# Expert weights loaded as pairs of tiles, one transfer each, on Trainium2

## The reference, cut to what matters

```python
def _moe_swiglu(h, router_w, router_b, w1, w3, w2):      # 8 experts, top 2, hidden width 2816
    logits = (h @ router_w).astype(jnp.float32) + router_b.astype(jnp.float32)
    top_vals, top_idx = lax.top_k(logits, TOP_K)
    ...
    for e in range(N_EXPERTS):
        out = out + gates[..., e:e + 1] * _swiglu(h, w1[e], w3[e], w2[e])
    return out
```

## Time and profile before

| what | value |
|---|---|
| device time, median of 3 runs | 4106.06 us (4105.6 to 4106.98) |
| the profiled execution, device time | 4107.23 us |
| its span, first to last instruction | 4105.4 us |
| mean granted TensorE clock | 0.922 |
| busy share PE, PEld, DVE, ACT | 87%, 75%, 66%, 49% |
| read from memory | 719.45 MB, 175 GB/s over the span |
| expert loads (`mraw`) | 726 of 512 KB, median 5.4 us to landing |

### The profile page before, as it was taken

One profiled execution on the slowest core, in us unless ns is written; L12 is line 12 of the kernel. 1 busy time (PEld: TensorE's weight loads), 2 busy tenths in 40 slices (PEclk: granted clock), 3 DMA queues, 4 the chain that ended last, 5 costly groups with the idle time before them and its releaser, 6 DMA issues.

```text
span 4105.4 us, 72288 instructions
## 1 busy us (share of the span) xinstructions
PE 3578.7 (87%) x27080; PEld 3085.1 (75%) x27080; DVE 2719.8 (66%) x3625; ACT 2028.4 (49%) x2685; POOL 145.8 (4%) x153
## 2 busy tenths in 40 slices
PE   7896629287999989899999999999997699997699
PEld 2374528286998976688888888887996599997598
DVE  6634765655555544789999999997556555555555
ACT  6622222212434433478888887886346244445343
POOL 0004900000000000000000000000000000000000
PEclk9897669699999999899999999999997699998699
DMA  9521000000454531179999999996542154543154
GB/s 354 211 87 46 1 6 3 1 3 30 147 182 153 180 138 52 66 258 360 365 363 360 364 360 363 360 362 223 182 159 92 47 184 154 189 157 109 46 169 159
DMA packets 199203, 723.08 MB, mean 176 GB/s; under 512 B 21872, under 2 KB 25328, under 8 KB 198640
## 3 DMA queue, kind: packets, MB, share of 16 engines
q1 hardware_dynamic: 198432, 713.89, 49.3%
q0 software_dynamic: 592, 6.69, 0.4%
HBM read 719.45 MB, written 1.05 MB: 175 GB/s over the span
## 4 chain that ended last, share of the span: by engine, by line
PE 80%; DVE 14%; ACT 3%; issue 1%; DMA 1%; SPq 0%; DVEq 0%; ACTq 0%; POOL 0%
PE ps L311 22%; PE ps L312 22%; PE ps L313 22%; PE ps L527 2%; DVE yc L2125 1%; PE ps L1268 1%; DMA ada_raw<-wstream 1%; PE ps L1265 1%; PE ps L1516 1%; PE ps L1533 1%; PE ps L1259 1%; PE ps L1848 1%; DVE rs L537 1%; PE ps L1797 1%; DVE normw L543 1%
## 5 line engine op out<-in xcount | busy, mean ns | idle before, releaser
L274 DVE TENSOR_TENSOR w_lo<-w_raw,w_hi 128x1024 fp32r<-128x1024 f32 x529 | 647.2, 1225 | 789.1 <-ACT w_hi L258 786.9
L311 PE MATMUL ps<-a_hi,w_hi 128*128 128x256 f32 (+1 forms) x3000 | 896.0, 299 | 94.0 <-DVE a_lo L1430 34.0
L258 ACT ACTIVATE w_hi<-w_raw 128x1024 fp32r<-128x1024 f32 x529 | 559.0, 1059 | 785.1 <-PE ps L313 762.1
L1933 DVE TENSOR_TENSOR mlo<-mraw,mhi 128x1024 fp32r<-128x1024 f32 x726 | 877.6, 1224 | 91.7 <-ACT mhi L1929 63.5
L312 PE MATMUL ps<-a_lo,w_hi 128*128 128x256 f32 (+1 forms) x3000 | 898.5, 299 | 0.0
L313 PE MATMUL ps<-a_hi,w_lo 128*128 128x256 f32 (+1 forms) x3000 | 896.0, 299 | 0.0
L1929 ACT ACTIVATE mhi<-mraw 128x1024 fp32r<-128x1024 f32 x726 | 770.7, 1062 | 180.7 <-PE ps L313 145.5
L311 PEld LDWEIGHTS ps<-a_hi,w_hi 128*128 128x128 f32 x3000 | 580.5, 194 | 120.2 <-issue 78.5
L313 PEld LDWEIGHTS ps<-a_hi,w_lo 128*128 128x128 f32 x3000 | 575.1, 192 | 16.2
L312 PEld LDWEIGHTS ps<-a_lo,w_hi 128*128 128x128 f32 x3000 | 574.4, 191 | 15.1
L311 PE MATMUL ps<-mhi,x_hi 128*128 128x512 f32 x968 | 395.9, 409 | 1.9 <-DVE mlo L1933 1.9
(11 more groups left out here) (489 smaller groups left out, 5226.3 us busy)
## 6 DMA issues: line engine op xcount, KB each, us to landing
mraw<-wexp SPq DMA_DIRECT2D x726, 512.0 KB, 5.4
w_raw<-wstream SPq DMA_DIRECT2D x529, 512.0 KB, 3.4
ada_raw<-wstream SPq DMA_DIRECT2D x96, 512.0 KB, 5.2
bia<-bias POOLq DMA_DIRECT2D x1, 4096.0 KB, 12.6
con<-consts SPq DMA_DIRECT2D x1, 1824.0 KB, 7.8
conb<-constsb POOLq DMA_DIRECT2D x1, 1224.0 KB, 7.5
hT<-ctxT SPq DMA_DIRECT2D x1, 1024.0 KB, 10.3
hT<-xT SPq DMA_DIRECT2D x1, 1024.0 KB, 12.5
```

Of the source, the lines that this page charges most:

```text
L258: nc.scalar.activation(whi[:, slot, :], raw[:, slot, :], ACT.Copy).then_inc(hi_ready.sem, 1)
L274: nc.vector.tensor_tensor(wlo[:, slot, :], raw[:, slot, :], whi[:, slot, :].bitcast(F32), ALU.subtract).then_inc(lo_ready.sem, 1)
L311: nc.tensor.matmul(out, lhs[0], rhs[0], start=start, stop=False, skip_group_check=skip)
L1933: nc.vector.tensor_tensor(mlo[:, slot, :], mraw[:, rslot, :], mhi[:, slot, :].bitcast(F32), ALU.subtract).then_inc(lo_ready.sem, 1)
```

## The change

The raw ring becomes three slots of two tiles (128 x 2048, 8 KB in a partition). One transfer of 1 MB loads a pair; its issue waits until DVE has finished both tiles of the pair that was there, and both tiles of a pair wait for the one semaphore of the slot. The host lays each two following tiles side by side. The bytes in SBUF, the bytes moved and the work of PE, ACT and DVE stay the same; 363 transfers take the place of 726.

```diff
-        mraw = sb("mraw", [P, MOE_RAW, 1024], at=x_at + 8 * KT * SLOTS)
+        mraw = sb("mraw", [P, MOE_RAW // 2, 2048], at=x_at + 8 * KT * SLOTS)
...
             def load(m, slot, idx):
                 if not (isinstance(m, int) and m < MOE_RAW):
-                    sp.wait_ge(lo_ready.sem, m + (BASE["moe"] - MOE_RAW + 1))
+                    sp.wait_ge(lo_ready.sem, m + (BASE["moe"] - MOE_RAW + 2))
                 sp.dma_start(mraw[:, slot, :], w[one(idx)].rearrange("o p c -> p (o c)")
                              ).then_inc(xraw[slot].sem, 16)
...
-                for q in range(4):
-                    load(m + q, (m + q) % MOE_RAW, e0 + q)
-                for q in range(2 if b else 0):
-                    load(m + 4 + q, (m + 4 + q) % MOE_RAW, before + (XT - 2 + q))
+                for q in range(2):
+                    load(m + 2 * q, (m // 2 + q) % (MOE_RAW // 2), e0 + q)
+                if b:
+                    load(m + 4, (m // 2 + 2) % (MOE_RAW // 2), before + (XT // 2 - 1))
                 with sp.Fori(0, NSTEP - 1) as i:
-                    for j in range(6):
-                        load(i * 6 + (b * XT + 4 + j), (4 + j) % MOE_RAW, i * 6 + (e0 + (4 + j)))
+                    for j in range(3):
+                        load(i * 6 + (b * XT + 4 + 2 * j), (2 + j) % (MOE_RAW // 2), i * 3 + (e0 + (2 + j)))
...
-            act.wait_ge(xraw[rslot].sem, rounds * 16 + (16 + ADA // ADA_RING * 16))
+            act.wait_ge(xraw[rslot // 2].sem, rounds * 16 + (16 + ADA // ADA_RING * 16))
             act.wait_ge(tile_used.sem, n)
-            nc.scalar.activation(mhi[:, slot, :], mraw[:, rslot, :], ACT.Copy).then_inc(hi_ready.sem, 1)
+            nc.scalar.activation(mhi[:, slot, :], mraw[:, rslot // 2, rslot % 2 * 1024:(rslot % 2 + 1) * 1024], ACT.Copy).then_inc(hi_ready.sem, 1)
...
-            nc.vector.tensor_tensor(mlo[:, slot, :], mraw[:, rslot, :], mhi[:, slot, :].bitcast(F32),
+            nc.vector.tensor_tensor(mlo[:, slot, :], mraw[:, rslot // 2, rslot % 2 * 1024:(rslot % 2 + 1) * 1024], mhi[:, slot, :].bitcast(F32),
                                     ALU.subtract).then_inc(lo_ready.sem, 1)
...
-    return np.concatenate(out + [o[-1]], 0)
+    out = np.concatenate(out + [o[-1]], 0)
+    return out.reshape(XT // 2, 2, P, D).transpose(0, 2, 1, 3).reshape(XT // 2, P, 2 * D)
```

More of the change, by code:

```diff
@@ L1664, in sp_experts @@
                 if b < NE:
-                    e0 = b * XT
+                    e0 = b * (XT // 2)
                 else:
@@ L1668, in sp_experts @@
                         sp.wait_ge(*S("overflow").next("sp"))
-                    e0 = sp.value_load(xi[0:1, b - NE:b - NE + 1], min_val=0, max_val=NE - 1) * XT
+                    e0 = sp.value_load(xi[0:1, b - NE:b - NE + 1], min_val=0, max_val=NE - 1) * (XT // 2)
                 m = b * XT - 2 if b else 0
-                for q in range(4):
-                    load(m + q, (m + q) % MOE_RAW, e0 + q)
-                for q in range(2 if b else 0):
-                    load(m + 4 + q, (m + 4 + q) % MOE_RAW, before + (XT - 2 + q))
+                for q in range(2):
+                    load(m + 2 * q, (m // 2 + q) % (MOE_RAW // 2), e0 + q)
+                if b:
+                    load(m + 4, (m // 2 + 2) % (MOE_RAW // 2), before + (XT // 2 - 1))
                 with sp.Fori(0, NSTEP - 1) as i:
-                    for j in range(6):
-                        load(i * 6 + (b * XT + 4 + j), (4 + j) % MOE_RAW, i * 6 + (e0 + (4 + j)))
+                    for j in range(3):
+                        load(i * 6 + (b * XT + 4 + 2 * j), (2 + j) % (MOE_RAW // 2), i * 3 + (e0 + (2 + j)))
                 before = e0
-            for q in range(2):
-                load(MOE - 2 + q, (4 + q) % MOE_RAW, before + (XT - 2 + q))
+            load(MOE - 2, 2, before + (XT // 2 - 1))
         def pe_router(pe):
```

## The result

The changed kernel takes 4152.48 us in the median (4150.7 to 4154.82, 4 runs) against 4106.36 us of the kernel before on the same chips (4105.6 to 4106.98, 4 runs). The ratio is 1.0112, 95% interval 1.0099 to 1.0124: 46 us slower. The forecast was 4176 us, 70 us slower.

What follows compares the result with a forecast made beforehand. PE was taken to set the expert stage's pace at 8.71 us a step; a pair's landing of 5.2 plus 4.1 us made it 9.3, and 119 x 0.59 = 70 us more gave 4176 us, range 4104 to 4295.

Steps and rivals of the forecast that it cites:

- the round: Expert stage: a raw slot's cycle from issue to issue, 8.0 us of an 8.71 us step before, 9.3 us after.
- The fixed part: Slot's round without landing: hand-overs of 0.15 and 0.1 us plus 3.8 us of ACT and DVE work, taken as 4.1 us.
- The limit for the landing: Expert stage: the pair's load stays hidden while its landing is under 8.71 - 4.1 = 4.6 us.
- the landing of 1 MB: L, a pair's time from issue to landing in the expert stage, taken as 5.2 us.
- the lone tiles: 512 KB loads in two other stretches, 3.2 and 4.2 us to land; their middle plus 1.28 us gave 5.0 us.
- The lower bound of 4.5: Landing of a pair at best: 3.2 us for a lone tile plus 1.28 us for the second 512 KB.
- Nothing else was to cost: Engine work and SP's issuing 0 us, the start 0 us, the end under 1 us; other stages the same.
- The spacing of the pairs: Expert stage loads: pairs issued 2.9 us apart and moving for 2.6 us, so they hardly queue behind each other.
- The signs: Expert stage trace if right: PE waits for mlo, ACT for even tiles' loads, blocks about 102 us apart, PE busy 93 to 95%.
- Hidden after all: Rival: the pair lands in 4.5 us and the step stays 8.6 to 8.7 us; 4102 to 4114 us, chance 0.16.
- The clock: Rival: PE's waits drop its clock to 1.2 GHz in half the steps, 4260 us; chance 0.06 together with the queue rival.
- The rival in which the queue of the loaded stage stays: Landing stays 6.7 us, step 10.8 us, 250 us more, 4356 us; chance 0.06 together with the clock rival.

Runs made afterwards that it cites:

- the joint landing alone: The kernel before, each tile's load issued as early as before, but the even tile's split also waits for the odd tile's landing; 4177.06 us, ratio 1.0178.
- The run with the gates moved: The changed kernel with the gate ahead of tile 0 and silu and product behind tile 3, on ACT and DVE; 4126.81 us, ratio 1.0053.

## Why the prediction was right, and where it was off

**What bounds the kernel, and the round**: right. The fixed part was worked out as 4.05 to 4.1 us from the trace of before; the chain shows 4.06 in the changed kernel and 4.03 with the joint landing alone. The 0.7 us that were said to be left in a round before are 0.77 in the mean. The limit for the landing, 4.6 us, is where the knee lies: a median of 4.5 us costs 7 us, one of 4.9 us costs 46. One refinement: the 8.71 us are a mean. The median round before is 8.58 us, and the step in which a block is spread (1.43 us more) makes up the rest, so in most steps the limit is nearer to 4.5.

**The term that was mis-sized** is the landing of 1 MB: "the middle of the lone tiles, (3.2 + 4.2) / 2 + 1.28 = 5.0, and 0.2 us for the load: 5.2 us". It was 4.9 us in the median and 5.13 in the mean. It is the mean that sets the pace here. By the median the sum would give 119 x 0.29 = 35 us, which is 11 us too few, because it leaves the late landings out. What makes a fifth of the pairs land late wasn't tried. For the two slots with the gate or silu between their tiles the means are 0.18 + 5.03 + 0.08 + 3.83 = 9.12 us; the forecast had 5.2 + 4.1 = 9.3. Of the 0.18 us between them 0.17 are the landing and 0.01 the rest, and 119 x 0.18 = 21 us are most of the 24 us by which the forecast was high.

The run with the gates moved shows what late landings cost by themselves. Its typical round in the chain is 8.53 us, just under PE's 8.58, and by its median landing of 4.8 us it would be hidden. But its mean landing is 5.06 and its mean round 8.87 us; 119 x (8.87 - 8.70) = 20 us is nearly all of its 21.

How L was put together was in part luck. No row stood for the 0.2 us "for the load", and the stretches of 3.2 and 4.2 us are from another stage. The runs give 3.8 us for 512 KB and 1.1 more for the second 512 KB in this stage, medians both, where 3.7, 1.28 and 0.2 were added. The lower bound of 4.5 was too low: nothing of 363 pairs landed under 4.6.

**Nothing else was to cost**: right. SP still waits for DVE for most of the stage (783 of 1000 us), its queue adds the same 0.18 us before an issue as it did, and the stage's 48 us are all of the 46 between the profiled executions (4153.25 and 4107.23), so the stages outside add nothing.

**The spacing of the pairs** was not as written. The text let them be issued 2.9 us apart, so that they hardly queue behind each other. They bunch: by the trace the medians between one issue and the next are 2.3, 3.7 and 2.9 us. The pair that comes 2.3 us behind another (tiles 4 and 5) lands in 5.33 us in the mean, the others in 5.03. It is also the pair without the gate, with 3.53 us of work in place of 3.83, and so it is not left behind. On ACT the bunching is seen as one long wait and two short ones in a step:

```profile
2206.11 1.06 ACT L1928 ACTIVATE mhi<-mraw 128x1024 fp32r<-128x1024 f32 x1 [1.50 <-DMA mraw<-wexp]
...
2208.55 1.06 ACT L1928 ACTIVATE mhi<-mraw 128x1024 fp32r<-128x1024 f32 x1 [0.16 <-DMA mraw<-wexp]
...
2211.14 2.03 ACT L1928 ACTIVATE mhi<-mraw 128x1024 fp32r<-128x1024 f32 x2 [0.31 <-DMA mraw<-wexp]
```

All three slots have the same mean round, 9.12 us.

**The signs** named in advance: PE waits for `mlo` (right), ACT waits for the load in 273 of 329 pairs (83%, "nearly every" forecast), blocks 100.3 us apart (102 forecast), transfers 345 GB/s (338 forecast), landing 4.9 (5.2 forecast). One sign was missed: PE's busy share is 97.7% and not 93 to 95%. The matmuls begun fell by 4.5%, but each one counts as busy for a little longer: 977.06 us over 4288 is 0.228 us, where 1000.00 over 4490 is 0.223.

**The rivals.** "Hidden after all" fell, but only just: with seven eighths of the bytes 7 us are left of the 46. The fit of the Trainium skill (DMA: Bandwidth & Descriptors, Anatomy of one DMA) is made for transfers issued by GpSimd; these loads are issued by SP, which the prediction left out. An estimate from it is 4.4 us for 1 MiB. The runs show 4.9 under this load and never less than 4.6, and that half a microsecond is the difference between hidden and 46 us. The clock stayed at 1.00. The rival in which the queue of the loaded stage stays (6.7 us) fell, as the landing got shorter and not longer than the 5.4 us of one tile. The same page of the Trainium skill (Rules for kernel authors) asks for at least 1 MiB in a transfer for bandwidth. That was no help here: the rate went down from 362 to 345 GB/s, since in this stage the rate follows the ring's round and not the size of the transfer.

## What to carry to other kernels

Write down the round of a buffer slot before its tiles are made larger: hand-over, landing of the whole transfer, and all the work that must be done on it before it is free, and compare it with the time in which the slot comes round again. With the same bytes of buffer, half as many slots of double size put the second tile's work into the round (1.36 us here), though no engine does more. The landing needn't grow against a ring that is full of smaller loads (5.13 us here, 5.39 before), so it is to be measured in the stage. Use its mean and not its median: with no reserve left, every late landing counts. When the round is over the pace, taking out what stands between the parts of one slot (here 0.33 us of a gate) saves time, as a shorter transfer does. With the round under the pace neither was worth anything here.

## What the runs showed of the hardware

A load of 1 MB landed sooner in this stage than a load of 512 KB had: 4.9 us against 5.4. The landing of 512 KB depends on how the loads are issued, at nearly the same rate in the stage. When each is issued by itself, every 1.45 us in the mean, it takes 5.4 us in the median (362 GB/s). When two are issued 0.53 us apart (361 GB/s), the first takes 3.6 to 4.1 us and the second 4.7 to 5.0, by slot, so that both have landed some 5.2 to 5.5 us behind the first issue. When half the bytes move it takes 3.8 us (181 GB/s). In steps from 512 to 1024 KB the landing grew by 0.4 us for 256 KB, 0.3 for the next 128 KB and 0.4 for the last. The busy share of the transfer engines fell from 0.98 to 0.96 with two together and to 0.91 with 1 MB transfers; the last is more than the 5% by which the rate fell. Why a stream of evenly spaced loads takes longest for each wasn't tried.
